# Reordering four places of a two-block float32 transformer kernel on one core

## What is computed

```python
# first block, two layers (a: sliding window with sinks, b: one block of 256, so plain causal attention)
for i in range(2):
    hn = rmsnorm(h, norm_g[i])
    q, k, v, z = split_proj(hn, w_in[i], n_kv)      # 16 heads of 64; 2 or 4 key heads
    o = attention(rope(q), rope(k), v)
    h = h + (o * silu(z)) @ w_out[i]
h = rmsnorm(h, final_g)
# second block, two hybrid layers
for layer in range(2):
    p = rmsnorm(h) @ w_in                            # q, k, v, z, xbc, dt
    attn = dilated attention, 8 heads
    y = chunked state-space scan of silu(conv(xbc)), * silu(z), normed in 2 groups
    h = h + concat(attn, y) @ w_out                  # 512 + 1024 wide
    h = h + (silu(rmsnorm(h) @ w_gate) * (rmsnorm(h) @ w_up)) @ w_down   # 2816 wide
out = rmsnorm(h, final_norm)
```

## Time and profile before

| | |
|---|---|
| median of 3 runs | 902.82 us (900.8 to 903.1) |
| the profiled execution: its own time | 902.35 us |
| its span, first to last instruction | 900.6 us |
| PE busy | 881.9 us (98%), 4570 matmuls |
| DVE busy | 557.6 us (62%) |
| ACT busy | 515.1 us (57%) |
| POOL busy | 132.6 us (15%) |
| read from HBM | 144.52 MB, 162 GB/s over the span |

### The profile page before, as it was taken

How to read it: one execution, slowest core, us unless ns; L and a number is a source line. 1 busy time by engine, 2 the same in 40 slices (tenths; PEclk the granted TensorE clock), 3 DMA queues, 4 the chain that set the end, 5 groups by cost and what they waited for, 6 DMA issues and landing times. The chain is left out here.

```text
span 900.6 us, 12331 instructions
## 1 busy us (share of the span) xinstructions
PE 881.9 (98%) x4570; PEld 726.1 (81%) x4570; DVE 557.6 (62%) x982; ACT 515.1 (57%) x849; POOL 132.6 (15%) x104
## 2 busy tenths in 40 slices
PE   7999999999999999999999999999999999999996
PEld 4878888788878888888888888888878888888885
DVE  5855776557767677765555545756678755555444
ACT  5676566765677775554444433668765644444332
POOL 0032124221033530000000000053430000000001
PEclk9999999999999999999999999999999999999999
DMA  8732455425354423766655554643334675555531
GB/s 300 241 101 93 140 188 186 141 70 168 121 184 141 138 97 112 231 219 187 187 187 186 187 187 146 208 137 106 133 123 147 202 222 185 183 185 184 189 110 47
DMA packets 94750, 146.36 MB, mean 163 GB/s; under 512 B 6500, under 2 KB 54884, under 8 KB 94692
## 3 DMA queue, kind: packets, MB, share of 16 engines
q1 hardware_dynamic: 92804, 139.52, 47.6%
q0 software_dynamic: 1296, 4.72, 1.7%
q10 hardware_dynamic: 592, 1.34, 0.5%
HBM read 144.52 MB, written 1.05 MB: 162 GB/s over the span
## 5 line engine op out<-in xcount | busy, mean ns | idle before, releaser
L978 DVE TENSOR_TENSOR lo<-raw,hi 128x1024 fp32r<-128x1024 f32 (+1 forms) x244 | 301.2, 1260 | 133.1 <-ACT hi L1286 130.9
L1286 ACT ACTIVATE hi<-raw 128x1024 fp32r<-128x1024 f32 (+1 forms) x260 | 266.6, 1057 | 81.4 <-PE bank L1118 77.2
L1118 PE MATMUL bank<-hi,xT_hi 128*128 128x512 f32 (+2 forms) x736 | 292.3, 397 | 4.8 <-DVE xT_lo L1724 3.0
L1118 PE MATMUL bank<-hi,xT_lo 128*128 128x512 f32 (+2 forms) x736 | 283.7, 385 | 0.0
L1118 PE MATMUL bank<-lo,xT_hi 128*128 128x512 f32 (+2 forms) x736 | 282.6, 384 | 0.0
L1118 PEld LDWEIGHTS bank<-hi,xT_hi 128*128 128x128 f32 x736 | 138.8, 189 | 37.7 <-issue 8.1
L1118 PEld LDWEIGHTS bank<-hi,xT_lo 128*128 128x128 f32 x736 | 138.5, 188 | 28.4
L1118 PEld LDWEIGHTS bank<-lo,xT_hi 128*128 128x128 f32 x736 | 139.0, 189 | 25.0 <-issue 0.5
L1118 PE MATMUL bank<-hi,hT 128*128 128x512 f32 x352 | 111.4, 395 | 0.0
L1118 PEld LDWEIGHTS bank<-hi,hT 128*128 128x128 f32 x352 | 66.3, 188 | 15.4
L1118 PE MATMUL bank<-lo,hT 128*128 128x512 f32 x176 | 69.4, 395 | 0.0
(11 more groups left out here) (243 smaller groups left out, 1026.9 us busy)
## 6 DMA issues: line engine op xcount, KB each, us to landing
raw<-in_w_in SPq DMA_DIRECT2D x26, 1024.0 KB, 5.0
raw<-in_w_gate SPq DMA_DIRECT2D x44, 512.0 KB, 4.0
raw<-in_w_up SPq DMA_DIRECT2D x44, 512.0 KB, 5.0
raw<-in_w_down SPq DMA_DIRECT2D x22, 1024.0 KB, 4.9
raw<-in_w_out SPq DMA_DIRECT2D x20, 1024.0 KB, 5.0
raw<-in_w_in_b SPq DMA_DIRECT2D x10, 1024.0 KB, 5.1
raw<-in_w_in_a SPq DMA_DIRECT2D x8, 1024.0 KB, 7.8
raw<-in_w_in_a SPq DMA_DIRECT2D x4, 256.0 KB, 5.0
```

Of the source, the lines that this page charges most:

```text
L978: return engine.tensor_tensor(lo[r][:, cols], raw[c.i % RAW][:, cols], hi[r][:, cols].bitcast(F32), ALU.subtract)
L1118: last = nc.tensor.matmul(bank[:, 0:wd], still[a], mv[r][:, off:off + wd], start=c.first and i == 0 and j == 0, stop=c.last and i == len(t ...
L1286: nc.scalar.activation(hi[c.i % SPLIT][:, cols], raw[c.i % RAW][:, cols], ACT.Copy)\
```

## The change

Four places are reordered. No arithmetic is added or taken away.

1. Attention slot 4 instead of slot 5 of layers a and b evicts its outputs by DVE (the other by ACT).
2. The start: the four pieces of chunk 0 become steps of their own and alternate with the first half of x (first_turn and first_split), and the second half of x is turned and its first rows split before chunk 1 is split (step "second_weights"), the other rows after it.
3. Between the blocks, the squares and the factor of the second norm move to the next slot.
4. In a hybrid layer, `turn_y(0, 0)` stands before `scanned(1, 1)` instead of behind it.

```diff
@@ -250,7 +250,7 @@
         for head in (2 * n - 4, 2 * n - 3):
             s = sc.step("pv", head=head, att=a, bank=a["obank"], p=a["base"] + head)
             a["pv"].append(s)
-        by_vector = (n == 5) if a["kind"] != "h" else n in (3, 5)
+        by_vector = (n == 4) if a["kind"] != "h" else n in (3, 5)
         o = sc.step("vector_oev" if by_vector else "oev", att=a, pair=head // 2, bank=a["obank"], pv=s)
         a["obank"].freed = (o, PARTS[o.kind][0])
         a["oev"].append(o)
@@ -325,18 +325,19 @@
 
     def factors():
         turn_x(sc, 1, 1)
+        squares(sc, 1)
         if mid:
-            squares(sc, 1)
             factor(sc, "first")
             normed_residual(sc)
-            squares(sc, 0)
-            squares(sc, 1)
-            factor(sc, "both")
         else:
-            squares(sc, 1)
             factor(sc, "h")
 
-    sc.soon += [second_half, factors]
+    def second_factor():
+        squares(sc, 0)
+        squares(sc, 1)
+        factor(sc, "both")
+
+    sc.soon += [second_half, factors] + [second_factor] * mid
 
 
 def normed_residual(sc):
@@ -625,7 +626,7 @@
 
     out_product(sc, w["out"], 12, {
         0: (do(decay, 1, 1, 0) + do(state, 1), do(decay, 1, 1, 1)),
-        1: (do(scanned, 1, 1) + do(turn_y, 0, 0), do(turn_y, 0, 1) + do(decay, 1, 0, 0) + do(decay, 1, 0, 1)),
+        1: (do(turn_y, 0, 0) + do(scanned, 1, 1), do(turn_y, 0, 1) + do(decay, 1, 0, 0) + do(decay, 1, 0, 1)),
         2: (do(scanned, 1, 0) + do(group_norm, 1) + do(next_gain), ()),
         3: (do(turn_y, 1, 0), do(turn_y, 1, 1))})
 
@@ -704,15 +705,21 @@
     bk = sc.bank()
     s = sc.step("columns", bank=bk)
     bk.freed = (s, "vector")
-    first = [first_turn(sc, 0, m) for m in range(M)]
-    first_split(sc, first[0])
-    sc.step("first_half")
-    first_split(sc, first[1])
+    first = first_turn(sc, 0, 0)
+    sc.step("piece")
+    first_split(sc, first)
+    sc.step("piece")
+    first = first_turn(sc, 0, 1)
+    sc.step("piece")
+    first_split(sc, first)
+    sc.step("piece")
     sc.step("begin")
 
     def second():
-        for x in [first_turn(sc, 1, m) for m in range(M)]:
-            first_split(sc, x)
+        first = [first_turn(sc, 1, m) for m in range(M)]
+        first_split(sc, first[0])
+        sc.step("second_weights")
+        first_split(sc, first[1])
         squares(sc, 0)
 
     sc.soon += [second, lambda: (squares(sc, 1), factor(sc, "h"))]
@@ -726,12 +733,12 @@
 
 def due(s):
 
-    if s.kind in ("first_half", "begin"):
-        return [(0, 0 if s.kind == "first_half" else 1)]
+    if s.kind == "second_weights":
+        return [(1, 0), (1, 1)]
     if s.due is not None:
         return s.due
     if s.i < 2:
-        return {("chunk", 0): [(1, 0), (1, 1)], ("rest", 0): [(2, 0)],
+        return {("chunk", 0): [], ("rest", 0): [(2, 0)],
                 ("chunk", 1): [(2, 1), (3, 0)], ("rest", 1): [(3, 1)]}[s.kind, s.i]
     return [(s.i + AHEAD, 0 if s.kind == "chunk" else 1)]
...
@@ -1268,15 +1275,6 @@
         def split(c, half):
-            if c.i == 0:
-
-                cw = c.size // 4
-                for k in (2 * half, 2 * half + 1):
-                    act.wait_ge(raw_first[k] if k < 3 else raw_in[0], 16)
-                    cols = slice(k * cw, (k + 1) * cw)
-                    nc.scalar.activation(hi[0][:, cols], raw[0][:, cols], ACT.Copy)\
-                      .then_inc(sem["chunk", "scalar"] if k % 2 else first_hi, 1)
-                return
             if half == 0:
...
+        def piece(k):
+            cw = chunks[0].size // 4
+            cols = slice(k * cw, (k + 1) * cw)
+            act.wait_ge(raw_first[k] if k < 3 else raw_in[0], 16)
+            nc.scalar.activation(hi[0][:, cols], raw[0][:, cols], ACT.Copy)\
+              .then_inc(sem["chunk", "scalar"] if k % 2 else first_hi, 1)
+
...
         for s in sc.steps:
-            if s.kind in ("first_half", "begin", "chunk", "rest"):
+            if s.kind in ("second_weights", "chunk", "rest"):
...
+            elif s.kind == "piece":
+                piece(s.i)
...
@@ -1595,19 +1602,18 @@
...
+        def piece(k):
+            cw = chunks[0].size // 4
+            cols = slice(k * cw, (k + 1) * cw)
+            dve.wait_ge(sem["chunk", "scalar"] if k % 2 else first_hi, k // 2 + 1)
+            tt(lo[0][:, cols], raw[0][:, cols], hi[0][:, cols].bitcast(F32), ALU.subtract)\
+                .then_inc(sem["chunk", "vector"] if k % 2 else first_lo, 1)
...
```

More of the change, by code:

```diff
@@ L1597, in split @@
         def split(c, half):
[L1598 to L1605, removed]
             dve.wait_ge(sem["chunk", "scalar"], 2 * c.i + half + 1)
```

## The result

The kernel with the change takes **895.38 us** (median of 6 executions, 895.14 to 895.81), the kernel before 902.77 (900.8 to 903.1) beside it. The ratio is 0.9922, with a 95% interval of 0.9909 to 0.9935: 7.4 us less by the medians. The profiled execution of after took 895.39, its span is 893.6; before it was 902.35 and 900.6. So the two profiled executions differ by 7.0, and that is what the sum of the prediction is held against.

A forecast was written before the change was run, and what follows sets the result against it. PE, busy 98% of the span, was taken as the bound, with 8.3 us of listed waits. Gains of 2.85 + 2.9 + 0.8 + 0.45 = 7.0 off the profiled 902.35 gave 895.4 us, range 893.6 to 899.3.

The forecast's parts named there:

- no wait at the start of the hybrid projection: Sign listed for the trace after the change: PE would not wait at all where the hybrid projection begins.
- Start: Program start: turning the second half of x before chunk 1 is split cuts PE's 3.0 us wait; net 2.85 us.
- 1.1 us later: Program start: with pieces of chunk 0 alternating with x, PE reaches the eight transposes at 12.8 instead of 11.68.
- new wait of 0.35: Chunk 2: its second half ends at 24.15 but PE wants it at 23.85; with the signal, 0.35 us of wait.
- Slots 4 and 5: Attention a and b: DVE evicts slot 4, ACT slot 5, so PE's eviction waits go; 2.5 and 0.4, sum 2.9 us.
- slot 5 waits in turn: Rival, chance 0.13: ACT evicts 0.8 us late in slot 5 of both layers, 1.6 come back, 897.0 us.
- Second norm: Between the blocks: DVE's lo and ACT's hi go ahead of the second middle norm's work; 0.8 us, bounds 0.5 and 0.8.
- y first: Both hybrid layers: oT_hi runs 5 us before, so PE's wait for turned y goes; 0.45 us, bounds 0 and 0.7.
- PE keeps about 0.2 of 0.36 each time: Hybrid layers: of each 0.36 us wait for turned y about 0.2 is won, since hyb_MT is late next.
- Lower level kept: Rival, chance 0.12: PE's clock falls behind one of the start's remaining gaps and costs 1.7 us as before, 897.1.
- It does nothing: Rival, chance 0.04: each wait goes to the next in line, 902 us.
- slower: Rival, chance 0.02: the lower clock level lasts through the start, chunks 0 and 1 take 10.9 us longer, 906.2.

The follow-up runs named there:

- The version with the decays first: Pieces of chunk 0 in their old order, and the two decays of group 0 ahead of the second turn of y, both hybrid layers, against the changed kernel: 893.97 us.

## Why the prediction was right

The forecast of 895.4 (893.6 to 899.3) held: 895.38. The sum of 7.0 is the 6.96 by which the last matmuls lead. But terms inside it were off and cancelled, so that it came out within 0.05 us is luck. One of its own signs of being wrong did show: "no wait at the start of the hybrid projection" was said, and a wait of 0.45 for hyb_q stands there.

**Start, 2.85 foretold, 2.94 measured.** The reading held: chunk 1 behind its own weights, at 16.89 (said 16.95); no low level; chunk 2 at 22.43 (22.4); its second half late next. Two sizes were off. "1.1 us later" for the alternation was 0.86, since DVE's first lo came at 7.21, where I had 7.55: ACT's piece 0 ran from 6.55 (said 6.9), when its weights had landed. And the "new wait of 0.35" in chunk 2 is 0.17 late by PE's timeline, 0.27 by what the version without it gained. With the alternation undone, 0.6 by the trace and 0.8 by the medians came back of its 0.86, so it was right to charge the start with it. The foretold wait of "near 2" for the pieces did not come: 0.4 is listed for them, with 0.7 for xT_lo ahead. And 2.94 is the best of five: in the other four kernels with this start chunk 3 begins at 28.50 to 29.01 in place of 28.45, a gain of 2.4 to 2.9 by this trace of before.

**Slots 4 and 5, 2.9 foretold, 3.06 measured** (1.25 and 0.32, 1.49 for both in layer b). The waits of 1.30 and 0.21 went, in both layers, and the margin of 0.15 held: the rival "slot 5 waits in turn" did not come. The pair that could have been named is the other one: with DVE kept in slot 5 the same wait would have grown from 0.21 to 1.23. So the two halves of this edit are not worth 2.5 and 0.4. Slot 4 by DVE alone gives 2.5 and loses 2.0 of them again in slot 5; the swap is one edit.

**Second norm, "0.8 us" foretold, 0.81 measured, but 0.38 of them at the place that I named.** The step that failed is that nothing stood behind lo. The matmul waits for several things, the list shows only the last, and the second to last was near. In before, ACT's timeline has it:

```profile
243.59 1.26 ACT L1360 ACTIVATE hyb_q<-bank,rms 128x512 f32<-128x512 f32 x2 [0.29 <-DVE rms L1756]
```

The first of these two ends at 244.27, against 244.69 for lo: with lo gone, only about 0.4 us was to be had. In after the same eviction begins at 237.58, and PE goes on at 238.41:

```profile
237.58 1.27 ACT L1367 ACTIVATE hyb_q<-bank,rms 128x512 f32<-128x512 f32 x2 [1.23 <-DVE rms L1764]
```

The other 0.43 came at the turned keys, where the wait of 0.23 for hyb_kdup went. I had only said that the keys "were 0.2 late already and move as DVE does", as a lower bound; the wait went, since on DVE one lo of 1.2 us fewer stands between the factor and the keys. The experiment with this part undone has all three back: lo 0.8, hyb_kdup 0.2, no hyb_q. The right sum had two errors of 0.4 in it, of opposite sign.

**y first, "0.45 us" foretold, 0.21 measured** (0.09 and 0.12). oT_lo's wait went, as said, and hyb_MT was late next, as said; the mis-sized term is "PE keeps about 0.2 of 0.36 each time". By the starts of matmuls, 0.5 was won at the first place (the lead goes from 6.81 to 7.32) and 0.42 given back at hyb_MT. The version with the decays first confirms both the cause and the size: it gets 0.39 of those 0.42 back.

**Lower level kept** (0.12) did not come in any of the six executions of after, by their mean clocks of 0.997 to 0.999. The 35 executions of before beside the experiments fall in two groups: eleven at a mean clock of 0.997 or 0.998, 900.3 to 901.3, and 24 at 0.994 to 0.996, 901.9 to 903.85. The medians, 900.9 and 902.6, are 1.7 apart, the 1.7 of the earlier trace rows. The Trainium skill (TensorE: Matmul & The Clock Gate, Part 1) says that the gate's watching runs freely and is not reset by a kernel's start. The two groups agree with that, but do not prove it, since no run shows the gate's own time. So of the 7.4 us between the medians of before and after, about 5.5 are waits removed in every execution and the rest is a level that came in two of three.

**It does nothing, and slower**: no sign of either. The granted clock was 1.00 over the whole stretch from 7 to 30 us, in spite of the gaps:

```profile
7.00:30.00 23.00, 21.16 (x115) 17.00 (x114) 18.64 (x31) 16.70 (x30) 1.38 (x2) 1.00 0.93 336
```

The columns are those of the windows above.

## What to carry to other kernels

Before a wait is counted as gain, read what else the waiting instruction needs, and when that is ready: the list of waits shows the last releaser only, and the second to last bounds what one gets. Move work that PE waits for ahead of work that nobody wants yet on the same in-order queue, but look at both engines: the copy that was right for DVE in slot 4 was wrong for it in slot 5, since there a lo that waits 2.9 us for ACT stands ahead. Measure such an edit by how much the lead grows at its own place, from the starts of the same matmuls in two traces. From chunk 3 to the last matmul the traces of after, of the kernel with the old pieces and of that with the old start take 857.15, 857.08 and 857.01 us, so about 0.1 can be told there, where medians resolve some 0.5. Ahead of chunk 3 two executions of the same start can differ by 0.6.

## What the runs showed of the hardware that was not expected

A short wait costs more than its bracket says. Matmuls of 512 columns last 0.39 by their modelled ends but start 0.23 apart, so the first 0.16 of a delay is not shown as idle; and the next start behind a wait comes 0.31 to 0.33 later, not 0.23 (16.89 and 17.20 in after, 18.47 and 18.80 in before). The same step stands without a wait where other work came between (343.41 and 343.72, behind the matmuls of hyb_MT, in the version with the decays first), so a wait adds it only in the middle of a run. The wait of 0.36 for oT_lo gave 0.51 when it went, hyb_MT's 0.17 gave 0.39. The waits of the scores, behind small transposes, were nearer to what they showed: 1.30 gave 1.25, and 0.21 gave 0.32.

The lower clock level came behind a wait of 3.0 us in some executions and, by their mean clocks, not in others of the same kernel, and once behind one of 1.3 us (the kernel with filler, at 66.65), where it did not stand in the profiled execution of before. In the profiled execution with the 3.0 us wait filled by matmuls that compute nothing the level did not come at that place, and 0.42 of wait was left; with the filler nine of eleven executions were free of the level by their mean clocks, against seven of seventeen without it on the same chip, and 11 of 35 over all. That this is the filler's doing and not chance is likely from these counts, but which executions get the level was not settled: no run controlled the state of the clock gate when the kernel began.

The scatter of a kernel without the low level lies mostly in its first 7 us. The five profiled executions with the new start reach the transposes at 12.54, 12.58, 12.90, 13.04 and 13.11, and their times are 0.01, 0.07, 0.37, 0.51 and 0.47 above the medians of their kernels.
